# Input tiles normalised and turned as they land, their splits inside the front block, and most parameter loads issued later

## The chip, the cores and the metric

The kernel runs on one core of one Trainium2 chip. The metric is the device time of one execution in microseconds (us); 2674.11 us is the median of three runs of the kernel before.

## The reference

A sequence of 512 rows of width 1024 passes through two blocks of a first model and one of a second. Only the beginning matters here. The first layer takes the input `x`, normalises each row by its root mean square and multiplies by a gain:

```python
h = _rmsnorm(x, norm_g[0, 0])        # x * rsqrt(mean(x*x) + 1e-6) * g
h = _ssd_mlstm_mixer(h, ab_w_in[0], ...)   # first: h @ w_in, 1024 x 7728
# of the product: z, xbc (conv of 5 taps, silu), dt_raw, q, k, v, o_pre, gates
```

`dt_raw` and `gates` are narrow parts of the product (32 columns each). They receive per-head biases and feed the decays of two scans. Everything after them (a mixer of two scans, a feed-forward net, a second layer with another scan, a second model with sparse attention, convolution, memory attention and 32 experts) is computed by code that the change leaves alone.

## The kernel before, in words

The rows lie on the partitions in four tiles of 128 rows (`k.x`, NT = 4). Products need them turned, with the 1024 columns on the partitions in eight chunks of 128 (KD = 8). A product in float32 is made of three products of a cheaper type: each operand is split into a high part (`hi`, a cast) and a remainder (`lo`, the whole less the high part), and hi*hi, lo*hi and hi*lo are summed in PSUM (function `product`, lines 384 to 386). Casts are made by ScalarE (ACT), remainders by VectorE (DVE), line 379 in the helper `rest`.

The start of the kernel is a row of blocks. At the end of a block all engines meet; each engine runs its own list of instructions in order.

1. `setup`, first block. SyncE (SP) issues the loads of the four input tiles, the first 2 MB of projection weights (`load_weights`, line 181), 12 parameter rows broadcast to all partitions (`brow`, line 248) and two loads of the narrow weights for dt and gates (`front_units`, line 250). It then waits until every parameter has landed and issues the second 2 MB. ACT issues 24 small parameter loads (line 261) into seven groups in `k.h`, and makes one root for all tiles. DVE squares and sums each tile as it lands (line 311), waits for the root, takes the reciprocal and scales the four tiles into `xn` (line 319). GpSimd (POOL) builds the identity and two triangles.
2. `setup`, second block. TensorE (PE) turns the seven parameter groups, a product with the identity each (line 285), and ACT copies them to `k.pcol` (line 292). Group 0 has the gains and the first convolution's taps and biases; groups 1 to 6 are used by later layers.
3. `norm_split`. PE turns the normalised input, 8 chunks by 4 tiles, 32 turns (line 1040), chunk by chunk into the eight PSUM banks; ACT casts each chunk times its gain to `h_hi` (line 1047), and DVE makes `h_lo` (line 1053).
4. `front`. PE runs three filling products (`fill_wait`, line 301) and the dtg product: 24 products of 64 rows of weights into bank 7, chunk by chunk. Then comes a stream of pieces p = 0, 1, 2, ..., each of 12 products of 512 columns for the 2 MB weight jobs of 8 pieces. Piece p needs its weights cast by ACT (line 997) and their remainder by DVE; both run two pieces ahead, in a ring of three places, and a place is free once PE has done piece p - 3. Other work is put between the pieces by number: ACT takes dt and gates out of bank 7 at p = 1, DVE makes the convolution of a finished tile at every odd p from 3 on (line 1395), the gate sums with the broadcast biases at p = 4 (`gates_in`, lines 1404 to 1410), a series for the logarithm at p = 6 to 10, and PE the cumulative sums at p = 13. SP loads the third job when DVE has finished the remainders of the first eight pieces. The row broadcast `gpost` of the first norm of a scan is used from p = 76 on.

The front runs on with further pieces up to p = 103; PSUM banks 0 to 3 take the pieces, banks 4 to 7 the work between them from p = 13 on.

Of the kernel before, what the change touches and what calls it, by code (L numbers as in the profile page):

```python
# [18 lines left out]
F32 = mybir.dt.float32  # L19
# [83 lines left out]
def everywhere(ap, n):  # L103

    return row(ap).to_broadcast([P, n])
# [91 lines left out]

def setup(k, first, xn, extra, extra_loaded):

# [24 lines left out]
    plan.append((6, 0, A["conv_w_2"][0].rearrange("t o (r c) -> (t o r) c", c=P)))  # L224
    used = [max(r + ap.shape[0] for g, r, ap in plan if g == n) for n in range(7)]

# [12 lines left out]
    rows_loaded = [k.new_count(f"input_loaded{t}") for t in range(NT)]  # L239

    with nc.Block(no_gpsimd_drain=True) as block:
        @block.sync
        def _(sp):
            for t in range(NT):
                sp.dma_start(k.x[:, t, :], A["x"][0, t * P:(t + 1) * P, :]).then_inc(rows_loaded[t].sem, 16)
            load_weights(k, sp, first[0])
            for dst, src in bplan:
                sp.dma_start(dst, src).then_inc(k.param_loaded.sem, 16)
            for dst, src in extra:
                sp.dma_start(dst, src).then_inc(extra_loaded.sem, 16)  # L250
            sp.wait_ge(*k.param_loaded(16 * (len(plan) + len(bplan))))
            load_weights(k, sp, first[1])

        @block.vector
        def _(dve):
            norm_rows(k, dve, k.x, xn, NT, rows_loaded)

        @block.scalar
        def _(act):
            for g, r, ap in plan:  # L260
                nc.scalar.dma_start(rows[r:r + ap.shape[0], g, :], ap).then_inc(k.param_loaded.sem, 16)
            norm_root(k, act, NT)

        @block.gpsimd
        def _(pool):
            nc.gpsimd.memset(k.ones[:, :], 1.0)
            nc.gpsimd.memset(k.eps[:, :], EPS)
            nc.gpsimd.memset(k.glr_raw[:, :, :], 0.0)
            pool.drain()

            nc.gpsimd.affine_select(out=k.ident[:, :], in_=k.ones[:, :], compare_op=ALU.is_equal, fill=0.0, base=0,
                                    pattern=[[1, P]], channel_multiplier=-1)
            nc.gpsimd.affine_select(out=k.tri[0][:, :], in_=k.ones[:, :], compare_op=ALU.is_ge, fill=0.0, base=0,
                                    pattern=[[1, P]], channel_multiplier=-1)
            nc.gpsimd.affine_select(out=k.tri[1][:, :], in_=k.ones[:, :], compare_op=ALU.is_ge, fill=0.0, base=0,
                                    pattern=[[-1, P]], channel_multiplier=1)
            pool.drain()
    k.param_loaded.close(16 * (len(plan) + len(bplan)))
    close_norm(k, NT)

    with nc.Block(no_gpsimd_drain=True) as block:
        @block.tensor
        def _(pe):
            for g in range(7):
                nc.tensor.transpose(k.ps[:, g, 0:used[g]], rows[0:used[g], g, :],
                                    k.ident[0:used[g], 0:used[g]]).then_inc(k.acc_ready.sem, 1)

        @block.scalar
        def _(act):
            for g in range(7):  # L290
                act.wait_ge(*k.acc_ready(g + 1))
                nc.scalar.copy(k.pcol[:, g, 0:used[g]], k.ps[:, g, 0:used[g]])
    k.acc_ready.close(7)

# [735 lines left out]

def norm_split(k, gain, h_hi, h_lo, xn):


    nc = k.nc
    with nc.Block(no_gpsimd_drain=True) as block:
        @block.tensor
        def _(pe):
            for c in range(KD):
                for t in range(NT):
                    last = nc.tensor.transpose(k.ps[:, c, t * P:(t + 1) * P], xn[:, t, c * P:(c + 1) * P], k.ident[:, :])  # L1040
                last.then_inc(k.acc_ready.sem, 1)

        @block.scalar
        def _(act):
            for c in range(KD):
                act.wait_ge(*k.acc_ready(c + 1))
                nc.scalar.activation(h_hi[:, c, :], k.ps[:, c, :], ACT.Copy, scale=gain[:, c:c + 1]).then_inc(k.h_hi_ready.sem, 1)

        @block.vector
        def _(dve):  # L1050
            for c in range(KD):
                dve.wait_ge(*k.h_hi_ready(c + 1))
                nc.vector.scalar_tensor_tensor(out=h_lo[:, c, :], in0=k.ps[:, c, :], scalar=gain[:, c:c + 1], in1=h_hi[:, c, :].bitcast(F32),
                                               op0=ALU.mult, op1=ALU.subtract)
    k.acc_ready.close(KD)
    k.h_hi_ready.close(KD)


def front(k, g, keep, b):

# [15 lines left out]

    dtg_loaded = b.dtg_loaded
    (dtg_hi, dtg_lo, small_cm, small_turned, small_ready, dec_v, dec_s, dec_p, conv_mid, conv_free, conv_ready, x_turned, x_read, b_turned, cb_done,
     cb_masked, xw_ready, st_done, st_upd, b_ready, arg_done, exp_done, w_ready, xdt_ready, y_done, i_done, i_free, y_free, skipped, gated, rooted,
# [56 lines left out]
    with nc.Block(no_gpsimd_drain=True) as block:  # L1136
        @block.sync
        def _(sp):
            sp.dma_start(k.gpost[:, :], everywhere(k.A["ab_ssd_norm"][0], D)).then_inc(gain_loaded.sem, 16)
            for p in range(NP + 1):  # L1140
# [23 lines left out]
        def _(pe):  # L1164
# [98 lines left out]

            fill_wait(k, NBANKS - 1, 3)
            pe.wait_ge(*dtg_lo(1))
            for c in range(KD):
                last = product(nc, k.ps[0:64, 7, :], [x[:, c, :] for x in b.dtg_w], [x[:, c, :] for x in (b.h_hi, b.h_lo)], c == 0, c == KD - 1)
            last.then_inc(k.products.sem, 1)
            for p in range(NP):
                st.group(pe, p, bank_free)  # L1270
                if p == 1:
                    pe.wait_ge(*small_cm(1))
                    for c in range(NT):
                        last = nc.tensor.transpose(k.ps[:, 6, c * 64:(c + 1) * 64], b.small_cm[0:64, chunk(c)], k.ident[0:64, 0:64])
                    last.then_inc(small_turned.sem, 1)
                if p == 13:
                    cumulate()
                if X_TURN <= p < X_TURN + NT:
                    turn_x(p - X_TURN)
                if p == B_TURN:  # L1280
                    turn_b()
                if p == CB:
                    scores()
                if STATES <= p < STATES + 6:
                    states(p - STATES)
                m = p - MIX
# [12 lines left out]
        def _(act):  # L1299
# [29 lines left out]

            act.wait_ge(dtg_loaded.sem, 32)  # L1330
            nc.scalar.copy(b.dtg_w[0][:, :, :], b.dtg_raw[:, :, :]).then_inc(dtg_hi.sem, 1)
            for p in range(LA):
                st.cast(act, p, 1)
            for p in range(NP + 1):
# [10 lines left out]
                if p >= 4 and p % 2 == 0 and (p - 4) // 2 < XT:  # L1345
                    tile_silu((p - 4) // 2)
                if p == 5:
                    act.wait_ge(*dec_v(1))
# [39 lines left out]
        def _(dve):  # L1388
# [173 lines left out]

            dve.wait_ge(*dtg_hi(1))
            rest(nc.vector, b.dtg_w[1][:, :, :], b.dtg_raw[:, :, :], b.dtg_w[0][:, :, :]).then_inc(dtg_lo.sem, 1)
            for d in DIRS:
# [60 lines left out]
    for sg in (k.pa, k.sa, k.vb):  # L1626
        sg.close(NT)


# [466 lines left out]
def layer0(k, next_gain, after):  # L2096
# [9 lines left out]
    with ExitStack() as layer:  # L2106
# [25 lines left out]
        with ExitStack() as e:  # L2132
# [25 lines left out]
            w = A["ab_w_in"][0].rearrange("(t p) n -> p t n", p=P)  # L2158
            setup(k, [job[0] for job in keep.jobs[:2]], k.ytmp,
                  [(b.dtg_raw[:, :, 0:32], w[:, :, DT0:DT0 + 32]), (b.dtg_raw[:, :, 32:64], w[:, :, G0:G0 + 32])], b.dtg_loaded)  # L2160
            norm_split(k, k.pcol[:, 0, 0:8], b.h_hi, b.h_lo, k.ytmp)
            front(k, g, keep, b)
        with ExitStack() as late:
# [2388 lines left out]
```

## Time and profile before

| | us |
|---|---|
| median of three runs | 2674.11 |
| lowest, highest | 2672.75, 2679.86 |
| the profiled execution's own time | 2675.97 |
| its span in the trace | 2674.1 |
| mean granted clock of TensorE | 0.978 |

The three runs and the profiled execution are executions of one program. The span is the time from the first to the last instruction of the trace. Busy time is that of an engine's instructions; register, branch, semaphore and DMA-issuing instructions don't count. A timeline row has its start, its length, the engine with the line and the operation, what is written and read, how many instructions it merges, and in brackets how long the engine was idle before and what released it. SPq and ACTq are the queues on which an engine issues DMAs; the length there is that of the issue, not of the transfer. The clock column is the share of 2.4 GHz that was granted to TensorE.

### The profile page before, as it was taken

To read this page: it belongs to the slowest core of one execution; us is meant where nothing else is said; L and a number is where in the kernel's file an instruction comes from. 1 tells how busy PE (TensorE), PEld (TensorE's weight loads), DVE (VectorE), ACT (ScalarE), POOL (GpSimd) and SP (SyncE) were. 2 spreads that over 40 slices of the span, in tenths; PEclk is the share of its full clock that TensorE was granted. 3 is DMA by queue.
4 is the path that set the end of the run, shared out by engine and by line. 5 is a ranking of instruction groups with operands and counts; after the bars stand their busy time and mean duration, and the time that the engine had idled before them with its cause. 6 is when DMAs were issued, how large, how long until landed. Compare 5 with 4: busy or idle time off the path is not lost. (4 is left out here: it accounts for less than half of the span.)

```text
span 2674.1 us, 32257 instructions
## 1 busy us (share of the span) xinstructions
PE 2504.2 (94%) x11397; PEld 1913.1 (72%) x11397; DVE 1591.4 (60%) x2349; ACT 1138.5 (43%) x1871; POOL 235.9 (9%) x239
## 2 busy tenths in 40 slices
PE   6999998789999999999999999999899899899995
PEld 5777786667888886766788888678757677666663
DVE  5766545654555534643555553538799646588884
ACT  3423342333444424623444442433333532377773
POOL 0000001000000000000000000255424000211111
PEclk9999999899999999999999999999999999899997
DMA  4222231031333412211233331322202014499995
GB/s 147 71 88 95 78 111 63 32 142 40 108 102 97 141 48 98 91 36 64 85 106 101 101 137 53 110 97 84 95 32 95 1 37 131 175 349 379 384 390 203
DMA packets 196719, 320.64 MB, mean 120 GB/s; under 512 B 16513, under 2 KB 112673, under 8 KB 196609
## 3 DMA queue, kind: packets, MB, share of 16 engines
q1 hardware_dynamic: 190992, 310.43, 33.5%
q0 software_dynamic: 4736, 8.40, 1.0%
q8 instruction: 69, 1.13, 0.2%
q10 hardware_dynamic: 881, 0.34, 0.0%
q14 instruction: 41, 0.34, 0.0%
HBM read 298.43 MB, written 29.10 MB: 122 GB/s over the span
## 5 line engine op out<-in xcount | busy, mean ns | idle before, releaser
L384 PE MATMUL ps<-ffn_parts 128*128 128x512 f32 x1056 | 411.6, 390 | 2.5 <-DVE ffn_parts L379 1.7
L386 PE MATMUL ps<-ffn_parts 128*128 128x512 f32 x1056 | 410.9, 389 | 0.0
L385 PE MATMUL ps<-ffn_parts 128*128 128x512 f32 x1056 | 410.8, 389 | 0.0
L384 PEld LDWEIGHTS ps<-ffn_parts 128*128 128x128 f32 x1056 | 198.2, 188 | 46.5 <-issue 2.6
L379 DVE TENSOR_TENSOR ffn_parts<-ring,ffn_parts 128x1024 fp32r<-128x1024 f32 x132 | 157.8, 1223 | 117.9 <-ACT ffn_parts L2406 107.4
L386 PEld LDWEIGHTS ps<-ffn_parts 128*128 128x128 f32 x1056 | 198.2, 188 | 41.2
L385 PEld LDWEIGHTS ps<-ffn_parts 128*128 128x128 f32 x1056 | 198.2, 188 | 41.1
L379 POOL TENSOR_TENSOR w_lo<-ring,w_hi 128x512 fp32r<-128x512 f32 (+1 forms) x112 | 160.6, 1438 | 720.4 <-ACT w_hi L543 720.0
L2457 DVE SCALAR_TENSOR_TENSOR y_tmp<-ps,pcol,y_tmp 128x511 f32<-128x511 f32 x88 | 61.9, 745 | 214.0 <-ACT y_tmp L2390 214.0
L997 ACT CAST front_w_hi<-ring 128x512 fp32r<-128x512 f32 x104 | 63.9, 618 | 219.7 <-PE ps L386 219.6
L379 DVE TENSOR_TENSOR front_w_lo<-ring,front_w_hi 128x512 fp32r<-128x512 f32 x104 | 71.5, 689 | 138.5 <-ACT front_w_hi L997 138.3
L543 ACT CAST w_hi<-ring 128x512 fp32r<-128x512 f32 (+1 forms) x112 | 68.3, 610 | 185.5 <-PE ps L386 178.1
L301 PE MATMUL ps<-brow,ident 128*128 128x512 f32 x240 | 121.8, 649 | 26.5 <-PEq L1899 6.1
L379 DVE TENSOR_TENSOR expert_up_lo<-ring,expert_up_hi 128x1024 fp32r<-128x1024 f32 x94 | 114.5, 1225 | 10.4 <-ACT expert_up_hi L4224 7.1
L3403 DVE SCALAR_TENSOR_TENSOR conv_gate<-conv_u,pcol,conv_gate 128x512 f32<-128x512 f32 x120 | 114.3, 1000 | 1.8
L2390 ACT ACTIVATE y_tmp<-ps,pcol 128x512 f32<-128x512 f32 x88 | 63.8, 775 | 109.7 <-PE ps L386 109.4
L4224 ACT CAST expert_up_hi<-ring 128x1024 fp32r<-128x1024 f32 x96 | 101.0, 1055 | 21.9 <-PE ps L386 18.9
L384 PE MATMUL ps<-kept_hi,w_hi 128*128 128x512 f32 x256 | 101.5, 397 | 3.8 <-POOL w_lo L379 2.5
L301 PEld LDWEIGHTS ps<-brow,ident 128*128 128x128 f32 x240 | 47.2, 207 | 79.4 <-issue 78.8
L384 PE MATMUL ps<-front_h_hi,front_w_hi 128*128 128x512 f32 (+1 forms) x232 | 97.5, 420 | 4.5 <-ACT hst L1328 2.7
L384 PE MATMUL ps<-wo_hi,lhs_hi 128*128 128x512 f32 x256 | 101.0, 395 | 0.2 <-DVE lhs_lo L379 0.2
L385 PE MATMUL ps<-kept_lo,w_hi 128*128 128x512 f32 x256 | 100.4, 392 | 0.0
(658 smaller groups left out, 5638.4 us busy)
## 6 DMA issues: line engine op xcount, KB each, us to landing
ring<-in_w_up SPq DMA_DIRECT2D x32, 1536.0 KB, 10.3
ring<-in_ffn_w_up SPq DMA_DIRECT2D x88, 512.0 KB, 5.0
moe_down<-in_w_down SPq DMA_DIRECT2D x32, 1024.0 KB, 11.0
ring<-in_ab_w_in SPq DMA_DIRECT2D x13, 2048.0 KB, 7.8
ring<-in_w_in SPq DMA_DIRECT2D x11, 2048.0 KB, 7.8
ring<-in_ffn_w_down SPq DMA_DIRECT2D x10, 2048.0 KB, 7.8
ring<-in_w_up SPq DMA_DIRECT2D x32, 512.0 KB, 11.2
ring<-in_c_w_in SPq DMA_DIRECT2D x6, 2048.0 KB, 8.0
```

Of the source, the lines that this page charges most:

```text
L301: k.nc.tensor.matmul(k.ps[:, bank, :], k.ident[:, :], k.brow[:, 0:BANK], start=True, stop=True)
L379: return engine.tensor_tensor(lo, whole, hi.bitcast(F32), ALU.subtract)
L384: nc.tensor.matmul(out, left[0], right[0], start=start, stop=False, **more)
L385: nc.tensor.matmul(out, left[0], right[1], start=False, stop=False, **more)
L386: return nc.tensor.matmul(out, left[1], right[0], start=False, stop=stop, **more)
L543: nc.scalar.copy(part(w_hi, p), chunk(j)[:, rows, cols]).then_inc(k.w_hi_ready.sem, 1)
L997: k.nc.scalar.copy(self.part(0, p), self.raw(p)).then_inc(k.w_hi_ready.sem, 1)
L2390: last = nc.scalar.activation(ybuf[:, s, half, :], bank(s, half), ACT.Identity, bias=column(bias, i, s, half), scale=column(tap1, i, s, half))
L2457: nc.vector.scalar_tensor_tensor(out=ybuf[:, s, half, 1:T], in0=bank(s, half)[:, 0:T - 1], scalar=column(tap0, i, s, half), in1=ybuf[:, s, ...
L3403: nc.vector.scalar_tensor_tensor(out=y[:, j, :], in0=u[:, j, i:i + T], scalar=tap[:, n:n + 1], in1=y[:, j, :], op0=ALU.mult, op1=ALU.add)
L4224: nc.scalar.copy(e.up_hi[:, 2 * q:2 * q + 2, :], up[s][:, 2 * q:2 * q + 2, :]).then_inc(e.up_cast, 1)
```

## The change

`setup` becomes `start`, a single block; its second block and `norm_split` are gone.

- Of the parameters only group 0 (8 loads, ACT) is loaded in `start`. The 12 broadcasts and the other 16 loads become `k.later`, and SP issues them at the head of `front`. DVE waits for all of them in `gates_in` (p = 4), PE before it turns groups 1 to 6 after piece 10; ACT copies those at p = 11.
- SP issues in `start`: input tiles, dtg weights, both weight jobs, without a wait.
- ACT takes a root of a constant first, then for each tile, once it has landed, the square with its sum and the root; DVE the reciprocal and the scaling of that tile alone.
- PE turns group 0 into bank 7 and then, tile by tile, chunks 0 to 6. Chunk 7 is turned in `front`, into bank 0, once `h_lo` of chunk 0 is made.
- The splits into `h_hi` and `h_lo` are the first thing that ACT and DVE do in `front`, with the cast and remainder of the dtg weights behind chunk 0. Two filling products instead of three are ahead of PE's chunk 7, and the dtg product waits chunk by chunk for `h_lo`.
- POOL clears `glr_raw` last instead of early.

```diff
@@ start (was setup)
+    now = [(rows[r:r + ap.shape[0], g, :], ap) for g, r, ap in plan if g == 0]
+    k.later = bplan + [(rows[r:r + ap.shape[0], g, :], ap) for g, r, ap in plan if g > 0]
         @block.sync
         def _(sp):
             for t in range(NT):
                 sp.dma_start(k.x[:, t, :], A["x"][0, t * P:(t + 1) * P, :]).then_inc(rows_loaded[t].sem, 16)
-            load_weights(k, sp, first[0])
-            for dst, src in bplan:
-                sp.dma_start(dst, src).then_inc(k.param_loaded.sem, 16)
             for dst, src in extra:
                 sp.dma_start(dst, src).then_inc(extra_loaded.sem, 16)
-            sp.wait_ge(*k.param_loaded(16 * (len(plan) + len(bplan))))
-            load_weights(k, sp, first[1])
+            for w in first:
+                load_weights(k, sp, w)
+        @block.tensor
+        def _(pe):
+            pe.wait_ge(*k.ga(1))
+            pe.wait_ge(*k.weights_loaded(16 * len(now)))
+            nc.tensor.transpose(k.ps[:, KD - 1, 0:used], rows[0:used, 0, :], k.ident[0:used, 0:used]).then_inc(k.acc_ready.sem, 1)
+            for t in range(NT):
+                pe.wait_ge(*k.norm_ready(t + 1))
+                for c in range(KD - 1):
+                    nc.tensor.transpose(k.ps[:, c, t * P:(t + 1) * P], xn[:, t, c * P:(c + 1) * P], k.ident[:, :])
         @block.vector
         def _(dve):
-            norm_rows(k, dve, k.x, xn, NT, rows_loaded)
+            for t in range(NT):
+                dve.wait_ge(*k.root_ready(t + 1))
+                nc.vector.reciprocal(rstd[:, t:t + 1], root[:, t:t + 1])
+                dve.drain()
+                nc.vector.tensor_scalar(xn[:, t, :], k.x[:, t, :], rstd[:, t:t + 1], None, ALU.mult).then_inc(k.norm_ready.sem, 1)
+                if t == 1:
+                    dve.wait_ge(*k.acc_ready(1))
+                    nc.vector.tensor_copy(k.pcol[:, 0, 0:used], k.ps[:, KD - 1, 0:used])
         @block.scalar
         def _(act):
-            for g, r, ap in plan:
-                nc.scalar.dma_start(rows[r:r + ap.shape[0], g, :], ap).then_inc(k.param_loaded.sem, 16)
-            norm_root(k, act, NT)
+            for dst, src in now:
+                nc.scalar.dma_start(dst, src).then_inc(k.weights_loaded.sem, 16)
+            act.wait_ge(*k.da(1))
+            nc.scalar.activation(k.stat[:, 3, 0:1], k.eps[:, 0:1], ACT.Sqrt)
+            for t in range(NT):
+                act.wait_ge(*rows_loaded[t](16))
+                nc.scalar.activation(xn[:, t, :], k.x[:, t, :], ACT.Square, accum_out=total[:, t:t + 1])
+                act.drain()
+                nc.scalar.activation(root[:, t:t + 1], total[:, t:t + 1], ACT.Sqrt, bias=k.eps[:, 0:1], scale=1.0 / D).then_inc(k.root_ready.sem, 1)
...
@@ front, sync
+            for dst, src in k.later:
+                sp.dma_start(dst, src).then_inc(k.param_loaded.sem, 16)
             sp.dma_start(k.gpost[:, :], everywhere(k.A["ab_ssd_norm"][0], D)).then_inc(gain_loaded.sem, 16)
@@ front, tensor
-            fill_wait(k, NBANKS - 1, 3)
+            for _ in range(2):
+                nc.tensor.matmul(k.ps[:, KD - 1, :], k.ident[:, :], xn[:, 0, 0:BANK], start=True, stop=True)
+            pe.wait_ge(*k.h_lo_ready(1))
+            for t in range(NT):
+                last = nc.tensor.transpose(turned_x(KD - 1)[:, t * P:(t + 1) * P], xn[:, t, (KD - 1) * P:], k.ident[:, :])
+            last.then_inc(k.pb.sem, 1)
             pe.wait_ge(*dtg_lo(1))
             for c in range(KD):
+                pe.wait_ge(*k.h_lo_ready(c + 1))
                 last = product(nc, k.ps[0:64, 7, :], ...)
...
+                if p == 10:
+                    pe.wait_ge(*k.param_loaded(later_loaded))
+                    for group in GROUPS:
+                        n = k.param_used[group[0]]
+                        last = nc.tensor.transpose(turned_params(*group), k.param_rows[0:n, group[0], :], k.ident[0:n, 0:n])
+                    last.then_inc(k.pb.sem, 1)
@@ front, scalar
+            for c in range(KD):
+                if c == KD - 1:
+                    act.wait_ge(*k.pb(1))
+                nc.scalar.activation(b.h_hi[:, c, :], turned_x(c), ACT.Copy, scale=gain[:, c:c + 1]).then_inc(k.h_hi_ready.sem, 1)
+                if c == 0:
+                    act.wait_ge(dtg_loaded.sem, 32)
+                    nc.scalar.copy(b.dtg_w[0][:, :, :], b.dtg_raw[:, :, :]).then_inc(dtg_hi.sem, 1)
...
+                if p == 11:
+                    act.wait_ge(*k.pb(2))
+                    for group in GROUPS:
+                        nc.scalar.copy(k.pcol[:, group[0], 0:k.param_used[group[0]]], turned_params(*group))
@@ front, vector
             def gates_in():
                 dve.wait_ge(*small_ready(1))
+                dve.wait_ge(*k.param_loaded(later_loaded))
...
+            for c in range(KD):
+                dve.wait_ge(*k.h_hi_ready(c + 1))
+                nc.vector.scalar_tensor_tensor(out=b.h_lo[:, c, :], in0=turned_x(c), scalar=gain[:, c:c + 1], in1=b.h_hi[:, c, :].bitcast(F32),
+                                               op0=ALU.mult, op1=ALU.subtract).then_inc(k.h_lo_ready.sem, 1)
+                if c == 0:
+                    dve.wait_ge(*dtg_hi(1))
+                    rest(nc.vector, b.dtg_w[1][:, :, :], b.dtg_raw[:, :, :], b.dtg_w[0][:, :, :]).then_inc(dtg_lo.sem, 1)
```

## Rows read from the trace of the kernel before

**Rows 1.** The page, busy time of each engine (share of the span) and instructions.

```profile
PE 2504.2 (94%) x11397; PEld 1913.1 (72%) x11397; DVE 1591.4 (60%) x2349; ACT 1138.5 (43%) x1871; POOL 235.9 (9%) x239
```

**Rows 2.** Stretches: us, busy PE PEld DVE ACT POOL (x), clock, DMA share, GB/s.

```profile
29.60:39.50 9.90, 9.83 (x31) 5.12 (x31) 2.30 (x5) 1.66 (x3) 0.00 (x0) 0.83 0.15 55
...
49.00:87.00 38.00, 34.89 (x157) 28.19 (x156) 33.40 (x62) 18.22 (x29) 0.00 (x0) 0.96 0.24 82
```

**Rows 3.** Timeline, 2 to 19 us: start, us, engine, line, out<-in, count, idle.

```profile
3.28 1.10 SPq L248 DMA_DIRECT2D brow<-in_ab_dt_bias  x1
3.62 0.37 ACTq L261 DMA_DIRECT2D h_cm<-in_ab_mlstm_norm  x1
...
4.42 1.81 SPq L248 DMA_DIRECT2D brow<-in_ab_fg_bias  x1
...
9.17 1.23 DVE L311 CUSTOM_DVE_ANT_0 y_tmp<-x_tm 128x1024 f32<-128x1024 f32 x1 [0.19 <-DMA x_tm<-in_x]
...
10.68 1.28 ACT L325 ACT_TABLE_LOAD   x1 [10.68 <-issue]
...
11.97 0.21 ACT L325 ACTIVATE stat<-stat 128x4 f32<-128x4 f32 x1
...
12.47 2.74 DVE L319 TENSOR_SCALAR y_tmp<-x_tm,stat 128x1024 f32<-128x1024 f32 x4
12.62 0.43 SPq L248 DMA_DIRECT2D brow<-in_b_rg  x1
...
13.57 3.35 SPq L250 DMA_DIRECT2D front_units<-in_ab_w_in  x2
18.39 0.37 SPq L181 DMA_DIRECT2D ring<-in_ab_w_in  x1
```

**Rows 4.** Landing of DMAs to 30 us: input tiles, weight loads, dtg loads.

```profile
DMA to landing us min/median/max: 3.4/5.1/7.0
...
DMA to landing us min/median/max: 7.7/10.3/13.0
...
DMA to landing us min/median/max: 5.2/5.3/5.5
```

**Rows 5.** Timeline, 19 to 40 us.

```profile
19.27 1.35 PE L285 MATMUL ps<-ident,h_cm 120*128 120x120 f32 x7 [19.27 <-PEq L241]
...
21.27 6.08 PE L1040 MATMUL ps<-ident,y_tmp 128*128 128x128 f32 x32 [0.65 <-PEq L281]
...
25.81 2.55 ACT L1047 ACTIVATE front_h_hi<-ps,pcol 128x512 fp32r<-128x512 f32 x4 [0.17 <-PE ps L1040]
...
27.90 1.40 DVE L1053 SCALAR_TENSOR_TENSOR front_h_lo<-ps,pcol,front_h_hi 128x512 fp32r<-128x512 f32 x2
...
29.67 4.47 PE L301 MATMUL ps<-brow,ident 128*128 128x512 f32 x6 [2.32 <-PEq L1035]
...
33.58 0.79 PE L384 MATMUL ps<-front_h_hi,front_w_hi 128*64 128x512 f32 x1
...
39.50 0.39 PE L384 MATMUL ps<-front_h_hi,front_w_hi 128*128 128x512 f32 x1
```

**Rows 6.** Busy time by stretch where the clock moves.

```profile
26.20:27.20 1.00, 1.00 (x11) 0.91 (x9) 0.90 (x2) 0.99 (x3) 0.00 (x0) 1.00 0.00 0
23.20:24.20 1.00, 1.00 (x7) 1.00 (x6) 0.90 (x2) 0.78 (x2) 0.00 (x0) 1.00 1.06 410
...
85.00:91.00 6.00, 6.00 (x17) 4.94 (x18) 1.72 (x3) 0.63 (x1) 0.00 (x0) 0.50 0.83 319
```

**Rows 7.** Timeline of ACT, a later norm of one tile, its square.

```profile
642.76 1.03 ACT L729 ACTIVATE q_region<-ps 128x1024 f32<-128x1024 f32 x1 [3.96 <-PE ps L386]
...
644.14 1.04 ACT L729 ACTIVATE q_region<-x_tm 128x1024 f32<-128x1024 f32 x1
```

**Rows 8.** Timeline of DVE at 53 us and of PE at 71 us.

```profile
53.83 0.29 DVE L1404 TENSOR_TENSOR q_region<-g_small,brow 128x128 f32<-128x128 f32 x1
...
71.34 0.50 PE L384 MATMUL ps<-front_h_hi,front_w_hi 128*128 128x512 f32 x1 [0.70 <-DVE front_w_lo L379]
```

More of the change, by code:

```diff
@@ L195, with start @@
 GATE_BIAS = 52
-def setup(k, first, xn, extra, extra_loaded):
+def start(k, first, xn, extra, extra_loaded):
     nc, A = k.nc, k.A
@@ L224, in setup @@
     plan.append((6, 0, A["conv_w_2"][0].rearrange("t o (r c) -> (t o r) c", c=P)))
-    used = [max(r + ap.shape[0] for g, r, ap in plan if g == n) for n in range(7)]
+    k.param_used = [max(r + ap.shape[0] for g, r, ap in plan if g == n) for n in range(7)]
     broad = [("ab_dt_bias", "a h -> (a h)"), ("ab_fg_bias", "a h -> (a h)"), ("ab_ig_bias", "a h -> (a h)"),
@@ L239, in setup @@
     rows_loaded = [k.new_count(f"input_loaded{t}") for t in range(NT)]
+    k.param_rows = rows
+    now = [(rows[r:r + ap.shape[0], g, :], ap) for g, r, ap in plan if g == 0]
+    k.later = bplan + [(rows[r:r + ap.shape[0], g, :], ap) for g, r, ap in plan if g > 0]
+    root, rstd, total = (k.stat[:, n, 0:NT] for n in range(3))
+    used = k.param_used[0]
     with nc.Block(no_gpsimd_drain=True) as block:
@@ L266, in _ @@
             nc.gpsimd.memset(k.ones[:, :], 1.0)
-            nc.gpsimd.memset(k.eps[:, :], EPS)
-            nc.gpsimd.memset(k.glr_raw[:, :, :], 0.0)
+            nc.gpsimd.memset(k.eps[:, :], EPS).then_inc(k.da.sem, 1)
             pool.drain()
             nc.gpsimd.affine_select(out=k.ident[:, :], in_=k.ones[:, :], compare_op=ALU.is_equal, fill=0.0, base=0,
-                                    pattern=[[1, P]], channel_multiplier=-1)
+                                    pattern=[[1, P]], channel_multiplier=-1).then_inc(k.ga.sem, 1)
             nc.gpsimd.affine_select(out=k.tri[0][:, :], in_=k.ones[:, :], compare_op=ALU.is_ge, fill=0.0, base=0,
@@ L276, in _ @@
                                     pattern=[[-1, P]], channel_multiplier=1)
+            nc.gpsimd.memset(k.glr_raw[:, :, :], 0.0)
             pool.drain()
[L278 to L293, printed above, removed]
+    k.weights_loaded.close(16 * len(now))
+    for s in (k.ga, k.da, k.acc_ready):
+        s.close(1)
+    for s in (k.root_ready, k.norm_ready):
+        s.close(NT)
 def fill_wait(k, bank, passes):
@@ L1028, in group, with front @@
         last.then_inc(k.products.sem, 1)
[L1031 to L1059, printed above, removed]
+def front(k, g, keep, b, xn):
     nc = k.nc
@@ L1077, in front, with turned_x, turned_params @@
     dtg_loaded = b.dtg_loaded
+    gain = k.pcol[:, 0, 0:KD]
+    later_loaded = 16 * len(k.later)
+    GROUPS = ((1, KD - 1, 0), (2, KD - 1, 1), (3, KD - 1, 2), (4, KD - 1, 3), (5, 4, 0), (6, 4, 1))
+    def turned_x(c):
+        return k.ps[:, c % (KD - 1), :]
+    def turned_params(g, bank, at):
+        n = k.param_used[g]
+        return k.ps[:, bank, at * P:at * P + n]
     (dtg_hi, dtg_lo, small_cm, small_turned, small_ready, dec_v, dec_s, dec_p, conv_mid, conv_free, conv_ready, x_turned, x_read, b_turned, cb_done,
@@ L1328, in evacuate @@
                 nc.scalar.activation(dst, st.bank(a), func, scale=scale).then_inc(k.acc_free.sem, 1)
-            act.wait_ge(dtg_loaded.sem, 32)
-            nc.scalar.copy(b.dtg_w[0][:, :, :], b.dtg_raw[:, :, :]).then_inc(dtg_hi.sem, 1)
+            for c in range(KD):
[5 more added lines that the diff above has]
+                    nc.scalar.copy(b.dtg_w[0][:, :, :], b.dtg_raw[:, :, :]).then_inc(dtg_hi.sem, 1)
             for p in range(LA):
@@ L1561, in norm @@
                 last.then_inc(normed.sem, 1)
-            dve.wait_ge(*dtg_hi(1))
-            rest(nc.vector, b.dtg_w[1][:, :, :], b.dtg_raw[:, :, :], b.dtg_w[0][:, :, :]).then_inc(dtg_lo.sem, 1)
+            for c in range(KD):
[5 more added lines that the diff above has]
+                    rest(nc.vector, b.dtg_w[1][:, :, :], b.dtg_raw[:, :, :], b.dtg_w[0][:, :, :]).then_inc(dtg_lo.sem, 1)
             for d in DIRS:
@@ L1627, in front @@
         sg.close(NT)
+    for sg in (k.h_hi_ready, k.h_lo_ready):
+        sg.close(KD)
+    k.pb.close(2)
+    k.param_loaded.close(later_loaded)
 MW = ML_D + 1
@@ L2158, in layer0 @@
             w = A["ab_w_in"][0].rearrange("(t p) n -> p t n", p=P)
-            setup(k, [job[0] for job in keep.jobs[:2]], k.ytmp,
+            start(k, [job[0] for job in keep.jobs[:2]], k.ytmp,
                   [(b.dtg_raw[:, :, 0:32], w[:, :, DT0:DT0 + 32]), (b.dtg_raw[:, :, 32:64], w[:, :, G0:G0 + 32])], b.dtg_loaded)
-            norm_split(k, k.pcol[:, 0, 0:8], b.h_hi, b.h_lo, k.ytmp)
-            front(k, g, keep, b)
+            front(k, g, keep, b, k.ytmp)
         with ExitStack() as late:
```

## The prediction

> **What bounds the kernel now.** I read the page's shares first: TensorE (PE) is busy 94% of the span [rows 1], so the time is PE's work plus the stretches in which PE has none. Next, where the first 87 us go, the only part the change touches. PE starts nothing before 19.27 us [rows 5]. From 29.6 to 39.5 us it is busy throughout, with three filling products and the small dtg product, at a mean clock of 0.83 [rows 2]. The projection's first piece starts at 39.50 us [rows 5]. From 49 to 87 us VectorE (DVE) is busy 33.40 of 38 us and PE 34.89, so there DVE sets the pace and PE waits a little [rows 2]. What moves the 39.50 us moves everything behind it, unless DVE or a DMA in the 49 to 87 us stretch is not moved along.
>
> The timeline shows why 39.50 is so late. The last input tile is squared at 9.17 us, one root for all four tiles follows at 11.97, the last scaling ends at 15.2, yet the first block does not end, because SyncE (SP) still issues: 12 row broadcasts from 3.28 to 13.57, then two dtg loads for 3.35 us, and then it waits for all parameters, to issue the second weight load at 18.39 [rows 3]. Seven parameter turns, 32 input turns, the splits and the fills come one block after the other [rows 5].
>
> **The change, part by part.** All times are of the profiled execution: its span is 2674.1 us, its own time 2675.97, the median of the three runs 2674.11. I subtract from the median.
>
> *Norm on landing.* ScalarE (ACT) now issues 8 parameter loads instead of 24; the eighth is issued by 4.0 us [rows 3]. Then a table load and a root, 1.28 + 0.21 = 1.5, so 5.5 us. A tile's square and root on ACT take 1.38 us from start to start [rows 7], and four end at 11.0; the fourth square starts at 9.6, after the last tile landed (9.17 at the latest, [rows 3]; 7.0 us after its issue at most, [rows 4]). DVE adds a reciprocal of 0.2 and one scaling, 2.74 / 4 = 0.7: 12.1. PE turned at 6.08 / 32 = 0.19 us each [rows 5]; seven turns of the last tile end at 13.4. The 28 turns from 8.0 us on would end at 13.3, so PE just keeps up. But PE turns the eight parameter loads first: with 3.4 us to land, the input's quickest, they are there at 7.4 and cost nothing; with 5.5, as the dtg loads had [rows 4], at 9.5, and the 28 turns end at 15.0, 1.6 later. DVE's copy of them stands behind tile 1 and beside the third root (9.6), so it holds little up. I take 7.4.
>
> *Joining.* Before, DVE's last split ended at 29.30 and the next block began at 29.64, thus 0.34 us; the front begins at 13.4 + 0.1 + 0.34, say 13.9. SP has long issued: two dtg loads (3.35 us) and two weight loads (0.5 each) after the input tiles end near 7. The 16 later parameter loads and 12 broadcasts are not waited for here.
>
> *Splits inside the front.* ACT's first split ends at 14.6. DVE then does eight remainders at 1.40 / 2 = 0.70 and the dtg remainder of 0.7, ending at 20.9, then two small subtractions (taken at 0.4 together, a quarter of a remainder's columns each) and the first weight remainder (0.7): 22.0. PE's own chain: two fills, two thirds of 33.58 - 29.67 = 3.91, are 2.6 (16.5), four turns 0.8 (17.3), and the 24 dtg products as before, 39.50 - 33.58 = 5.9 [rows 5]: 23.2. With PE at full rate a turn takes 1/11 us [rows 6] and a fill, two instructions of four times the columns, 0.73: 1.5 + 0.4 + 5.9 ends at 21.7, and DVE's 22.0 binds. At half rate throughout it is twice that, 15.6, ending at 29.5. I take 23.2, which is what the rows show for this very sequence; ends 22.0 and 29.5.
>
> *First weights.* They are now issued behind the dtg loads. First load before: 13.0 us to landing with the input ahead of it, alone 7.7 [rows 4]. Issued at 6.5, it lands at 14.2 to 19.5; ACT casts it at 19.5, after the eight splits at 0.64 (2.55 / 4, [rows 5]) and the dtg cast. If both 2 MB loads interleave instead, they land together: the input and one load, 4 MB, had landed by 2.7 + 13.0 = 15.7, and 2 MB more at that pace is 7.5: 23.2, and with a cast and a remainder the first piece starts at 24.5. I take no wait. The second is not needed before piece 8.
>
> *Later parameters.* SP issues 28 loads from 13.9 on. By the rows of the same loads, 12 broadcasts take 10.3 us (3.28 to 13.57) and the 16 others at most 10.68 - 4.0 = 6.7 [rows 3]: issued by 30.9, landed by 36.4 with 5.5 more. DVE waits for them before its gate sums, which ran at 53.83 [rows 8], 14.3 after the first piece, so now at 37.5. It has 1.1 us to spare, or 5.6 if a broadcast costs 0.48 instead of 0.86, as it did once ACT had stopped issuing (0.43 and a gap, [rows 3]). Cost: 0. Behind the waiting gate sums stands the next weight remainder, on which PE's piece 7 waits; a late landing is paid one for one. SP's next own duty, the third weight load, comes when piece 7 is split, about 40, after these issues; the ssd_norm load is not used before step 76.
>
> *Their turns.* Six turns at 0.19 = 1.2 us on PE after piece 10. There PE waited 0.70 us for DVE anyway before piece 11, and again before piece 12 (one of the two rows stands, [rows 8]). Ends: 0 and 1.2; taken 0.2. Six ACT copies, at most 0.69 each (the split's length, an upper end, 4.1 us); ACT is 18.22 of 38 us busy there [rows 2], so 0.
>
> *Sum:* 39.5 - 23.2 - 0.2 = 16.1 us. 2674.1 - 16.1 = **2658.0 us**.
>
> **Two rules of the Trainium skill.** The rows show that ACT's first activation follows its table load at once: load at 10.68 for 1.28, root at 11.97 [rows 3]. "ScalarE: Activation LUTs" (What ACT_TABLE_LOAD costs) adds a drain of about 1.38 us to each load. By the trace there is none; by the page the norm chain, which now hangs on this load, would end 1.4 us later, and the time be 2659.4. That lies in the forecast's own range and holds 0.05 of its chance.
>
> The clock column says 1.00 at 23.2 to 24.2, but PE made 7 turns there and 11 in 26.2 to 27.2 [rows 6]: PE starts at the lower level (1.2 GHz) and rises to 2.4 GHz only after it has worked, about 26 us. It fell again after the idle stretch from 27.4 to 29.67, and the fills ran low. "TensorE: Matmul & The Clock Gate" (The HAM clock gate) says the low rate is the default and activity lifts it; that speaks against starting the dtg product early, since a chain paced by DVE leaves PE gaps. It is rival 1.
>
> **Rivals.**
> 1. *PE stays low through the dtg product*, because it is fed in pieces by DVE. For: the drop at 29.7 after 2.3 us of idling [rows 2]. Against: it would now have turned since 8 us almost without a gap. First piece at 29.5, gain 9.8: **2664.3**. Chance 0.12.
> 2. *A low spell downstream comes or goes.* From 85 to 91 us PE ran at 0.50 [rows 6], behind its waits for DVE and narrow products. With the parameter turns in one of those gaps, and all else shifted, it may not come: some 6.6 us at half rate, worth 3.3, **2654.7**; an extra one gives 2661.3. Against: its cause, the waits and the narrow products, stays. Chance 0.16.
> 3. *The weights bind instead* (interleaved landing, piece 0 at 24.5, and a parameter wait of 3 us): gain 39.5 - 24.5 - 0.2 - 3 = 11.8, **2662.3**. Chance 0.08. If the eight parameter loads are late besides, or anything else keeps the first block open until less than 8 us is gained, it counts as no change (2667): 0.04.
> 4. *Slower: SP's issues grow.* One broadcast issue took 1.81 us while transfers were queued [rows 3]. If all 28 did so, with two weight loads queued ahead of them, they would end at 13.9 + 50.7 = 64.6, landed 70.1; the gate sums wait 32.6 us and PE with them: 2674.1 - 16.1 + 32.6 = **2690.6**. With 5.5 us to land, a wait begins from (32.0 - 13.9) / 28 = 0.65 us an issue, and the change loses from (48.1 - 13.9) / 28 = 1.22; I reckon with 17.0 / 28 = 0.61. Against: the last four broadcasts were at 0.43 to 0.44 (one of them stands, [rows 3]), with transfers queued too. Chance 0.02.
>
> **How the numbers follow.** The forecast holds 0.58 (its own range 2655 to 2661.5: a first piece from 22.0 to 24.5, and some 2 us for what runs differ by). The range 2650 to 2666 takes in rivals 1 to 3 and the 3 us by which runs of the same kernel differ. A measurement can tell about 0.3%, 8 us, from no change: 2666.1. Faster: 0.58 + 0.12 + 0.16 + 0.08 less a little for noise in rival 1 = 0.92; within: 0.06; slower: 0.02.
>
> **What would show it.** Right: input turns on PE beginning near 8 us and ending near 13.4; the front's first split near 14; the first piece of the projection at 22 to 24.5; no wait of DVE at the gate sums; the stretch from the first piece to 87 us as long as before; the remaining kernel of equal length. Wrong: ACT's squares later than 5.5 us, an idle DVE at its gate sums released by a broadcast, a cast waiting for the ring, the clock at 0.50 during the dtg product, or a first piece before 22 us.

## The result and the profile after

The changed kernel takes 2659.94 us (median, 2657.23 to 2661.43), where the kernel before took 2675.2 in the runs beside it: a ratio of 0.9944, 95% interval 0.9930 to 0.9958. The forecast was 2658.0, in a range of 2650 to 2666. A second set of runs of the same kernel gave 2664.1 and 0.9956 (0.9942 to 0.9970). The profiled execution has a span of 2659.4 us, 14.7 less than before.

The page's row of busy times, of the changed kernel, answers to [rows 1]:

```profile
PE 2503.9 (94%) x11395; PEld 1911.9 (72%) x11395; DVE 1586.5 (60%) x2344; ACT 1142.9 (43%) x1882; POOL 235.2 (9%) x239
```

PE's work is as long as before, within 0.3 us: the 14.7 us are idle time and not work. The timeline of the changed kernel to the first piece answers to [rows 3, 5]:

```profile
3.71 0.35 ACTq L281 DMA_DIRECT2D h_cm<-in_ab_mlstm_norm  x1
4.09 1.28 ACT L283 ACT_TABLE_LOAD   x1 [4.09 <-issue]
4.85 4.21 SPq L181 DMA_DIRECT2D ring<-in_ab_w_in  x2
5.38 0.20 ACT L283 ACTIVATE stat<-eps 128x1 f32<-128x1 f32 x1
5.49 1.04 ACT L286 ACTIVATE y_tmp<-x_tm 128x1024 f32<-128x1024 f32 x1
...
7.26 0.75 DVE L273 TENSOR_SCALAR y_tmp<-x_tm,stat 128x1024 f32<-128x1024 f32 x1
...
9.61 0.43 PE L261 MATMUL ps<-ident,h_cm 120*128 120x120 f32 x1 [9.61 <-DMA h_cm<-in_ab_mlstm_norm]
...
9.83 6.02 PE L265 MATMUL ps<-ident,y_tmp 128*128 128x128 f32 x28
...
11.47 0.75 DVE L273 TENSOR_SCALAR y_tmp<-x_tm,stat 128x1024 f32<-128x1024 f32 x1
...
16.24 0.69 ACT L1346 ACTIVATE front_h_hi<-ps,pcol 128x512 fp32r<-128x512 f32 x1 [5.04 <-PEq L247]
16.27 1.96 PE L1266 MATMUL ps<-y_tmp,ident 128*128 128x512 f32 x4 [0.41 <-PEq L247]
...
18.23 4.70 DVE L1588 SCALAR_TENSOR_TENSOR front_h_lo<-ps,pcol,front_h_hi 128x512 fp32r<-128x512 f32 x7
...
18.41 0.47 PE L399 MATMUL ps<-front_h_hi,front_w_hi 128*64 128x512 f32 x1
...
21.34 1.19 ACT L1012 CAST front_w_hi<-ring 128x512 fp32r<-128x512 f32 x2
...
23.24 1.29 DVE L394 TENSOR_TENSOR front_w_lo<-ring,front_w_hi 128x512 fp32r<-128x512 f32 x2
...
23.98 0.19 PEld L399 LDWEIGHTS ps<-front_h_hi,front_w_hi 128*128 128x128 f32 x1 [0.30 <-DVE front_w_lo L394]
24.00 0.47 PE L399 MATMUL ps<-front_h_hi,front_w_hi 128*128 128x512 f32 x1
```

ACT starts its norm at 4.09 and no longer at 10.68 us, the last tile is scaled at 12.2 (15.2 before), the front's first split starts at 16.24, and the first piece at 24.00 instead of 39.50: 15.5 us earlier. What released the first piece is DVE's first weight remainder (23.24 and some 0.7 us long), on which the weight load of 23.98 waited; PE's own products before it, 0.23 us apart, ended at the same moment. The same kernel by stretch (columns as in [rows 2]):

```profile
16.20:24.00 7.80, 7.74 (x32) 4.36 (x33) 7.04 (x13) 6.29 (x11) 0.00 (x0) 1.00 0.74 246
24.00:33.50 9.50, 9.50 (x44) 7.63 (x44) 2.60 (x4) 3.73 (x7) 0.00 (x0) 1.00 0.30 95
33.50:71.50 38.00, 35.50 (x170) 28.91 (x170) 33.40 (x62) 19.14 (x35) 0.00 (x0) 1.00 0.25 84
69.00:76.00 7.00, 7.00 (x35) 5.84 (x35) 4.72 (x7) 2.19 (x4) 0.00 (x0) 1.00 0.75 284
```

The stretch from 33.50 to 71.50 lies as far from the first piece as 49 to 87 before, and DVE is busy in it to the hundredth as long, 33.40 us. The fourth row lies 45 to 52 us behind the first piece, as 84 to 91 us did before, and its clock is 1.00: the low spell of [rows 6] did not come.

How much earlier the changed kernel is, at an instruction of DVE that both traces have, except for PE's first piece and the end (its start before less its start after; worked out from the two traces):

```
time before, us   earlier by, us
39.5 (PE, first piece)  15.5
92                      19.0
338                     17.4
1099                    18.0
1500                    18.1
2067                    17.2
2201                    16.4
2302                    14.6
2369                    13.9
end                     14.7
```

All of the gain is there at 39.5 us. Part of what it does afterwards, up and down by 1 to 4 us, coincides with low spells of PE's clock (stretches at a granted clock of 0.50): one of 6.8 us at 84 is missing after the change (+3.5), one of 3.4 us at 316 is new (-1.6), and in the stage from 2180 to 2330 us (2197 to 2347 before) there are 41.0 us of them instead of 30.7. The loss of 1.7 us between 1500 and 2201 us coincides with none: both traces have the same low spells there, 6.8 and 3.4 us. Its cause is open. Over the whole span the low spells sum to 117.4 us before and 116.9 us after.

### The profile page after: what moved, and what is told of

It reads as the page before. It is cut to its first block and busy times, and to the rows that moved or that the text cites. A ratio compares the mean times of both kernels' runs of the same rounds, so it can differ in the third digit from the quotient of the medians.

```text
span 2659.4 us, 32240 instructions
## 1 busy us (share of the span) xinstructions
PE 2503.9 (94%) x11395; PEld 1911.9 (72%) x11395; DVE 1586.5 (60%) x2344; ACT 1142.9 (43%) x1882; POOL 235.2 (9%) x239
```

## Experiments

In all of them the first piece and the front's start are read from the profile, since runs of one kernel differ by 3 to 11 us. Beside times stand the ratio to the kernel before and its 95% interval. Edits are shown shortened and in part in words, against the changed kernel unless it says otherwise.

**e1: the parameter loads as before.**

```diff
-            for dst, src in extra: sp.dma_start(dst, src)...
-            for w in first: load_weights(k, sp, w)
+            load_weights(k, sp, first[0])
+            for dst, src in bplan: sp.dma_start(dst, src)...
+            for dst, src in extra: sp.dma_start(dst, src)...
+            sp.wait_ge(*k.param_loaded(16 * len(k.later)))
+            load_weights(k, sp, first[1])
@@ scalar: the other 16 loads right behind the first 8; front: none
```

> The changed kernel with its parameter loads as before: ACT issues all 24, SP puts the 12 broadcasts between the first weight load and the dtg loads, waits for all parameters and then issues the second weight load. Norm by tile, splits in the front and the late turns stay. Theory A (the gain is a sum: block held open by the loads, splits as a block of their own, one root for all tiles): ACT's table load starts near 10.7 us instead of 4.1, roots end near 17.7, PE's turns near 19.7, the front begins near 20.0 instead of 16.24 and the first piece at 27.8 instead of 24.00; time about 2664 where the changed kernel has 2660. Theory B (all of the gain is the loads that held the block): the first piece returns to 39 us and the time to 2675.

2667.38 us, 0.9971 (0.9958 to 0.9983). First piece at 27.96 us, 4.0 later than in the changed kernel, by theory A 3.8. PE's timeline:

```profile
14.60 3.94 PE L268 MATMUL ps<-ident,y_tmp 128*128 128x128 f32 x21 [4.58 <-DVE y_tmp L276]
...
20.21 1.96 PE L1269 MATMUL ps<-y_tmp,ident 128*128 128x512 f32 x4 [0.41 <-PEq L247]
```

The front's fills begin at 20.21 instead of 16.27. The loads alone are 4 us of the 15.5; theory B, which wanted them to be all of it, falls. With the norm by tile and the splits in the front, it is ACT's late start (table load at 10.62) that leads here, since PE's last turns end at 19.79; SP's wait for parameters ends at 18.57, 1.2 us ahead of that. Which of the two alone would have left how much was not tried. The time is 7.2 us longer than the changed kernel's by the ratios, and 3.4 us above what theory A gave. The first piece explains 4.0 of it; the rest lies within the two intervals.

**e2: the splits as a block of their own.**

```diff
+    with nc.Block(no_gpsimd_drain=True) as block:   # ahead of the front
+        tensor: wait h_lo_ready(1), 4 turns of chunk 7
+        scalar: the 8 splits;  vector: the 8 remainders
     front: dtg cast, remainder and products as in the change
```

> The changed kernel with its eight splits into high and low parts, and the four turns of chunk 7, in a block of their own between start and front; the dtg cast, remainder and products follow in the front as before. Theory A: the splits' block runs from 16.24 to 22.7, the front begins at 23.0, two fills (2.0 us) and 24 products (5.9) follow, the first piece starts at 30.9 instead of 24.00, time about 2667. Theory B: the splits were hidden by nothing and cost nothing to separate, first piece within 1 us of 24.00, time 2660.

2667.57 us, 0.9968 (0.9954 to 0.9981). First piece at 31.44, 7.4 us later (theory A: 6.9). PE's timeline, and the stretch with the fills by busy time and clock:

```profile
21.57 2.90 PE L1288 MATMUL ps<-y_tmp,ident 128*128 128x512 f32 x3 [4.28 <-PEq L1135]
...
31.44 0.39 PE L399 MATMUL ps<-front_h_hi,front_w_hi 128*128 128x512 f32 x1
...
20.20:27.00 6.80, 5.43 (x9) 2.44 (x10) 3.28 (x7) 1.66 (x3) 0.00 (x0) 0.51 0.17 45
```

PE waits 4.3 us for the block's end, as it had 2.3 us before, and then its fills and first products run at a clock of 0.51. So a block of its own costs its length and also a low spell. This is the largest of the three parts, and 7.4 us is less than it costs from where it starts. Here PE's 28 turns took 4.82 us and not 6.02, so the first block ended 1.1 us earlier than in the changed kernel:

```profile
9.89 4.82 PE L265 MATMUL ps<-ident,y_tmp 128*128 128x128 f32 x28
...
15.10 4.73 ACT L1148 ACTIVATE front_h_hi<-ps,pcol 128x512 fp32r<-128x512 f32 x8 [3.81 <-PEq L247]
...
16.63 0.66 PE L1140 MATMUL ps<-ident,y_tmp 128*128 128x128 f32 x4 [1.91 <-DVE front_h_lo L1154]
```

From the first split to the first piece it is 16.3 us (15.10 to 31.44) where the changed kernel has 7.8 (16.24 to 24.00).

**e3: one root for all tiles.**

```diff
-            for t in range(NT): root, reciprocal and scaling of tile t
+            norm_rows(k, dve, k.x, xn, NT, rows_loaded)   # and norm_root on ACT
```

> The changed kernel with the norm as before: DVE squares the tiles as they land, one root for all, then four scalings; PE turns each tile as it is scaled. Theory A: DVE's squares end near 10.2, the root near 10.7 (its table is loaded already), scalings 11.0 to 13.8, 28 turns of 0.21 us from 11.8 to 17.8 since PE is still at its low clock; the front begins at 18.2 instead of 16.24 and the first piece at 26.0; time about 2662. Rival C (PE's slow turns and not the norm set the block's end): the front begins less than 1 us later than 16.24.

2661.23 us, 0.9949 (0.9931 to 0.9968). PE's timeline:

```profile
12.22 6.02 PE L265 MATMUL ps<-ident,y_tmp 128*128 128x128 f32 x28 [2.40 <-DVE y_tmp L324]
18.66 1.96 PE L1256 MATMUL ps<-y_tmp,ident 128*128 128x512 f32 x4 [0.41 <-PEq L247]
```

The front starts 2.4 us later than with the norm by tile, the first piece, at 26.39, too (theory A: 2.0). Rival C falls. The last squaring waited for its tile (9.40 us), then came root and four scalings in a row.

The three parts are 4.0 + 7.4 + 2.4 = 13.8 of 15.5 us. Each was undone with the others in place, so the sum need not close; the third fill less is some 0.9 more, an estimate from the 1.79 us that two fills take, which no run undid. Each part is one profile less another, and the changed kernel's own first piece lay at 24.00, 23.73 (e7) and 22.57 us (e6), so a part is known to about 1.4 us.

**e4: PE turns the parameters behind the second tile.**

```diff
-            wait for the 8 loads, turn group 0;  then the tiles
             for t in range(NT):
                 ...
+                if t == 1: wait for the 8 loads, turn group 0
@@ vector: copy of group 0 behind tile 3 instead of tile 1
```

> The changed kernel with PE's turn of parameter group 0 moved behind the second input tile's turns, and DVE's copy of it behind the fourth scaling. In the changed kernel PE first waited until 9.61 us for the small loads, while the first scaled tile was there at 8.0. Theory A (that wait is what put the front 2.3 us later than predicted): turns from 8.0, block end near 14.9, front at 14.9 instead of 16.24, first piece at 22.6 instead of 24.00, time about 2658.5. Rival D (PE's rise to the full clock decides: it comes after a fixed amount of turning): turns from 8.0, but the front and the first piece move by less than 0.5 us, because the fills and products then run at the low clock for as much longer.

2658.35 us, 0.9939 (0.9920 to 0.9959). PE's timeline:

```profile
8.14 3.22 PE L263 MATMUL ps<-ident,y_tmp 128*128 128x128 f32 x14 [8.14 <-DVE y_tmp L274]
11.16 0.40 PE L266 MATMUL ps<-ident,h_cm 120*128 120x120 f32 x1
11.36 2.19 PE L263 MATMUL ps<-ident,y_tmp 128*128 128x128 f32 x14
13.96 1.96 PE L1267 MATMUL ps<-y_tmp,ident 128*128 128x512 f32 x4 [0.41 <-PEq L247]
```

PE turns from 8.14 us instead of 9.83, its turns 15 to 28 take 2.19 us instead of 3.22, and the first piece starts at 21.71, 2.3 us earlier than in the changed kernel. 1.7 of that is the earlier start. The rest is the moment at which PE's turns become faster, and that moves between executions: in e6, whose start is the changed kernel's, PE turned from 9.71 on, but

```profile
9.71 4.67 PE L265 MATMUL ps<-ident,y_tmp 128*128 128x128 f32 x28
```

in 4.67 us instead of 6.02, and the front began at 14.77. By that run as the yardstick, e4 is 0.9 us earlier, not 2.3. Theory A gave 1.4 us for the first piece, and the two yardsticks lie on either side of it. Rival D falls all the same: the first piece moved by more than 0.5 us, and the two fills took 1.79 us as in the changed kernel. The time, 2658.35, is what theory A gave (2658.5), but the interval does not part it from the changed kernel's.

**e5: e4 with PE at work before the input is there.**

```diff
             pe.wait_ge(*k.ga(1))
+            for _ in range(16):
+                nc.tensor.matmul(k.ps[:, KD - 1, 0:P], k.ident[:, :], k.ident[:, :], start=True, stop=True)
```

> The kernel of the late parameter turn (e4) with 16 products of the identity with itself on PE between the identity's making (1.6 us) and the first scaled tile (8.1). In e4 PE's turns ran at 0.21 us each from 8.14 to about 12.4 and at 0.11 after it. Theory A (PE has to be at work to get the full clock, and it may be before the input is there): the products take 0.43 us each at first, the 28 turns run at 0.11 us, PE keeps up with DVE and the last tile's turns end near 13.0 instead of 13.55; front at 13.4 instead of 13.93, first piece at 21.2 instead of 21.71; time about 2657.5. Rival: the products are too light or too early, turns still at 0.21 us, and the front is not earlier than 13.9.

2661.65 us, 0.9953 (0.9938 to 0.9968); the profiled span is 2653.3 us, the shortest of all profiles, but that execution is the fastest of four (2655.15 us; the others 2660.24 to 2664.06). PE's timeline:

```profile
1.61 6.00 PE L261 MATMUL ps<-ident 128*128 128x128 f32 x32 [1.61 <-POOL ident L299]
8.11 0.99 PE L265 MATMUL ps<-ident,y_tmp 128*128 128x128 f32 x7 [0.49 <-DVE y_tmp L276]
...
12.32 0.98 PE L265 MATMUL ps<-ident,y_tmp 128*128 128x128 f32 x7 [0.42 <-DVE y_tmp L276]
13.71 1.95 PE L1269 MATMUL ps<-y_tmp,ident 128*128 128x512 f32 x4 [0.41 <-PEq L247]
```

Seven turns take 0.98 us, with 0.4 us of waiting for DVE between two tiles: now the norm by tile sets the block's end, and PE no longer does. Theory A holds and the rival falls. But the first piece comes at 21.47, only 0.24 us before e4's, since the last tile is scaled at 12.2 us in both, and its turns end at 13.30 here and at 13.55 in e4. The time was forecast at 2657.5; it is not told from e4's or from the changed kernel's.

**e6: the 28 late loads twice.**

```diff
+            for again in range(2):
+                if again: sp.wait_ge(*k.param_loaded(16 * len(k.later)))
                 for dst, src in k.later: ...
-    later_loaded = 16 * len(k.later)
+    later_loaded = 32 * len(k.later)
```

> The changed kernel with SP's 28 late loads issued twice (the second time after all of the first have landed), and the gate sums waiting for both. In the changed kernel they were issued from 16.23 to 27.57 us and the gate sums ran at 38.50. Theory A (a late landing is paid one for one by DVE and PE): first pass landed near 30, second issued by 41.5 and landed near 44, gate sums at 44 instead of 38.50, the stretch behind them 5.5 us later, time about 2665.5. Rival E (DVE has slack and catches up before PE needs it): gate sums at 44, but the convolution of tile 15 and all behind it less than 2 us later, time 2660 to 2662.

2665.44 us, 0.9967 (0.9952 to 0.9982). SP's last late load and DVE's gate sums:

```profile
41.77 0.30 SPq L1142 DMA_DIRECT2D h_cm<-in_conv_w  x1
...
44.25 0.29 DVE L1430 TENSOR_TENSOR q_region<-g_small,brow 128x128 f32<-128x128 f32 x1 [7.37 <-DMA h_cm<-in_conv_w]
```

DVE waited 7.37 us. Up to there this kernel was 16.9 us ahead of the kernel before, right behind it 9.6, and 10.0 from 56 us on: 6.9 of the 7.4 us waited stay lost. Rival E falls. The wait itself was longer than expected (44.25 against a point of 36.9 without it) because the first piece was early, at 22.57; the landing was as expected. The last load was there 2.2 us after its issue had ended.

**e7: the changed kernel again.**

> The changed kernel once more, unaltered, for a second profile. The low spell of PE's clock at 84 us before (6.8 us) was absent after the change, came at 72.4 us (6.8 us) with held parameters, at 72.7 and 67.2 us (3.4 us) in e3 and e4, and not in e2, though all of these turn the parameters after piece 10. Theory F (where the spells fall is the execution's affair: a phase of the clock against the kernel): a second profile of the same kernel shows other spells, and its span differs by the halves of their lengths, 1 to 4 us, with the first piece again at 24.0. Rival G (the spells belong to the kernel): the same list of spells within 1 us, none near 68 us.

2664.1 us, 0.9956 (0.9942 to 0.9970). PE's turns, and a stretch 46 us behind the first piece (23.73):

```profile
9.96 5.61 PE L265 MATMUL ps<-ident,y_tmp 128*128 128x128 f32 x28
...
69.50:73.20 3.70, 3.70 (x10) 2.86 (x10) 1.24 (x2) 0.63 (x1) 0.00 (x0) 0.55 1.05 404
```

Here the spell is back (0.55 from 69.5 to 73.2 us), in the kernel that had none near 70 us before. Its low spells sum to 124.2 us and its span is 2662.6: 7.3 us more at the low clock, of which half is 3.7, and a span longer by 3.2. Rival G falls: the list of spells is not the kernel's alone. Theory F holds in that the spells and the span change between executions of one program, but not in full. The places return: of the ten profiles kept, eight have a low spell that starts 44 to 46 us behind the first piece (in e6, 7.4 us of waiting left out), of 3.4 or 6.8 us, and only the first profile of the changed kernel and e2 have none. So the kernel sets where a spell can come, and the execution whether it does. Nor does half of the spells give the time in general: at 1244 us this execution was 5.8 us behind the first one with 20.5 us more of low spells.

**e8: e4 without the two fills.**

```diff
-            for _ in range(2):
-                nc.tensor.matmul(k.ps[:, KD - 1, :], k.ident[:, :], xn[:, 0, 0:BANK], start=True, stop=True)
```

> The kernel e4 without the two filling products at the head of the front. Theory A (PE has turned for 5 us just before and stays at the full clock): the turns of chunk 7 start at DVE's first remainder, near 15.4 instead of 15.75, and the first piece at 21.4 instead of 21.71. Rival (the fills keep the clock up): PE idle from 13.5 to 15.4 us, clock at 0.50 for at least 3.4 us of the dtg product, first piece at 23 or later.

2659.07 us, 0.9939 (0.9924 to 0.9954). PE's turns of chunk 7, and a stretch of the dtg product:

```profile
15.46 0.92 PE L1268 MATMUL ps<-ident,y_tmp 128*128 128x128 f32 x4 [1.91 <-DVE front_h_lo L1587]
...
16.00:19.40 3.40, 3.40 (x11) 1.87 (x10) 3.40 (x7) 3.40 (x7) 0.00 (x0) 0.54 1.05 387
```

PE was idle for 1.91 us, and from 16.0 to 19.4 us it ran at 0.54. The first piece starts at 23.06, 1.35 us later than with the fills, though DVE's first weight remainder begins at 20.93 in both. My theory A fell and the rival was right: two products that compute nothing start the first piece 1.35 us earlier, because they stand in a wait. In the time this does not show (2659.07 against 2658.35, with the same ratio). And the same pause does not always do it: in e2 PE also idled for 1.91 us ahead of the turns of chunk 7, and its clock stayed up behind it, until the next pause:

```profile
16.60:19.90 3.30, 0.66 (x4) 0.42 (x4) 3.30 (x6) 3.23 (x6) 0.00 (x0) 1.00 1.05 387
```

## Why the prediction was right

It was right in sum, 16.1 us forecast against 15.3 (medians) and 14.7 (spans), and by the mechanism it named: the first piece moves, 23.2 forecast and 24.00 found, and all behind it moves along. That the first piece came within 0.8 us is in part luck: one step was 2.3 us too early and the next 1.5 us too long. Two of the signs that it named did not come: the input turns ran from 9.83 to 15.85 and not from near 8 to near 13.4, and the front's first split was at 16.24 and not near 14. By its steps:

- *Norm on landing.* ACT's first activation was at 5.38, forecast 5.3; last scaling ended at 12.2, forecast 12.1. Right. The table load at 4.09 was again followed at once, at 5.38, so there is no drain of about 1.38 us such as the Trainium skill has in "ScalarE: Activation LUTs" (What ACT_TABLE_LOAD costs); the measurement decides, here and in [rows 3].
- *PE's turns.* Wrong by 2.3 us: I took 7.4 us for the landing of the eight small loads; it was 9.61, the upper end that I had named. I also took 0.19 us a turn, the mean over 32 turns of which the last were faster ([rows 6]). The 28 took 6.02 us, 0.215 each; e5 shows 0.14 for PE already at work. So the block ended at 15.9 and the front began at 16.24, not 13.9.
- *From the front's start to the first piece.* 7.8 us, forecast 9.3. The fills were taken as at a partly low clock (2.6 us), but took 1.8, the four turns 0.35 (0.8) and the 24 products 5.6 (5.9): PE had paused for only 0.41 us ahead of the fills, where it had paused for 2.3 before, and its clock stayed up. So I had chosen the wrong one of my two chains. I took PE's, with the low spell of before in it; what released the first piece is DVE's, level with PE's, as I had named it for PE at full rate (8.1 us after the front's start, measured 7.7). The two misses are independent: from the front's first split to the first piece it is 7.8 us in all seven profiles that keep the splits and the fills in the front, whether the 28 turns had taken 6.02 us or 4.67 (e6). It is luck that they had opposite signs. Rival 1 did not come, and e2 and e8 show what it looks like when PE's clock does fall ahead of the product.
- *First weights.* They landed 11.2 and 12.9 us after their issue, and ACT cast the first of them at 21.34, right behind its splits: no wait, as forecast. Their two issues took 4.21 us, where I had reckoned with 0.5 each; SP was done at 9.06, long before the block's end.
- *Later parameters.* Issued from 16.23 to 27.57, 0.40 us each where I had reckoned with 0.61, DVE's gate sums without a wait for them:

```profile
16.23 0.34 SPq L1139 DMA_DIRECT2D brow<-in_ab_dt_bias  x1
...
27.27 0.30 SPq L1139 DMA_DIRECT2D h_cm<-in_conv_w  x1
...
38.50 0.29 DVE L1427 TENSOR_TENSOR q_region<-g_small,brow 128x128 f32<-128x128 f32 x1 [0.17 <-issue]
```

  The slow broadcasts of before (up to 1.81 us) fell in the time in which SP and ACT both issued, or right behind it; that this is their cause is not shown. SP's second weight issue, behind the first in the 4.21 us above, took 3.58 us though ACT issued nothing. Rival 4's mechanism is real (e6), its price per us waited is right, but SP alone is far from it: 28 loads take 11.3 us.
- *Their turns.* 0.64 us on PE and 0.91 on ACT; I had 1.2 and at most 4.1. They lie in PE's wait; what was 0.70 us of waiting is 0.20, and the next wait, 0.92 us as before (then at 75.27), is untouched:

```profile
54.72 0.64 PE L1287 MATMUL ps<-ident,h_cm 88*128 88x88 f32 x6
55.56 0.50 PE L399 MATMUL ps<-front_h_hi,front_w_hi 128*128 128x512 f32 x1 [0.20 <-DVE front_w_lo L394]
...
59.92 0.91 ACT L1368 COPY pcol<-ps 128x88 f32<-128x88 f32 x6
```

- *Rival 2.* The spell at 84 us did not come, as that rival said, and its 3.5 us were there at 92 us; but others came later and the sum of low spells stayed. Its reason, the turns in a gap of PE, is refuted by e1 and e3, which turn at the same place and have a spell, and by e7, which is the same kernel and has one.

What stays open is why the clock's spells come in one execution and not in another, and the rest of the sum: e3 and e4 had 18 and 10 us less of low spells than the changed kernel, yet their spans are only 1.5 and 3.3 us shorter, e3 with a first piece 2.4 us later and e4 with one 2.3 us earlier. That a low spell costs its half only where PE binds would fit this, but at which of the later spells it does was not tried. Whether e4 or e5 beat the changed kernel in time is not shown either: they start the first piece 2.3 to 2.5 us earlier, and the intervals of the times are wider than that.

## What to carry to other kernels

A prologue's price is the time until the bound engine's first steady instruction: read it from the timeline, undo one part at a time, and compare that moment, since a few us are not seen in the total. Put work that belongs to no one before the barrier behind it, but compute the issue time of what is moved for the queue it goes to, and the moment of its first reader: where that reader sets the pace, nearly all of its wait is paid (6.9 of 7.4 us in e6). And keep TensorE turning or filling in a wait of 2 us ahead of dense products: in e8 leaving it idle cost 1.35 us.

## What the runs showed of the hardware

- TensorE with work from the identity on (1.6 us) made seven turns in 0.98 us (e5); without, 28 took 6.02, thus 1.5 for seven, at a clock column of 1.00 in both. At the start that column does not tell the clock, and the rate of turns does (as in [rows 6]).
- An idle stretch of 1.91 us, right behind turns, was followed by 3.4 us at half the clock in e8, but not in e2, where the clock fell only in the next pause, of 4.28 us. One of 0.41 us in the other kernels was not followed by a fall.
- From the same start, PE's turns became faster at another moment in each execution: 28 of them took 6.02, 5.61, 4.82 and 4.67 us in four executions whose first block is the same (the changed kernel, e7, e2, e6).
- The same program had 116.9 and 124.2 us of low clock in two executions, and spans that differ by 3.2 us.
- The last of eight small loads on ACT's queue, 4 KB, issued at 3.71 us, when four input tiles of 512 KB had been issued on SP's, was waited for until 9.61; in five other profiles until 9.39 to 9.73. In e6 the last of SP's late loads, 62 KB, was there 2.2 us after its issue had ended.
